# A four-layer diffusion step on one core: three more weight units outside the ring, half an adaLN third in layer 1, the first combine between gate and up, attention's second halves as Q, Q, K, K

## The chip, the core and the metric

The kernel runs on one core of a Trainium2 chip. TensorE (PE in the profile) does the matmuls and transposes, VectorE (DVE) and ScalarE (ACT) the elementwise work, GpSimd (POOL) and SyncE (SP) issue transfers. The metric is device time in microseconds of one execution.

## The reference, cut to what matters

Two sequences of 128 tokens with 1024 channels (context and latent) pass through four layers. Layer i has one token mixer (0 and 3: pooling, 1: attention with 16 heads, 2: Fourier mixing) and then a mixture of 16 experts, of which each token uses two of one group of four. Both are pre-normed and modulated by six rows of 1024 that a product of SiLU(cond) with `ada_w[i]` gives (adaLN).

```python
mod = (cond_act @ ada_w[i] + ada_b[i])[:, None, :]
sh1, sc1, g1, sh2, sc2, g2 = [mod[..., n * D:(n + 1) * D] for n in range(6)]
h = rms_norm(x, norm1_g[i]) * (1 + sc1) + sh1
m = pool_mix(...) or na_context/na_latent(...) or fourier_mix(...)
x = x + g1 * m
h = rms_norm(x, norm2_g[i]) * (1 + sc2) + sh2
x = x + g2 * moe(h, router_w, router_b, moe_w_gate[i], moe_w_up[i], moe_w_down[i])
```

All weights are float32: 24 MB of adaLN a layer, 16 MB for attention in all, and 96 MB of experts a layer. Every weight is read once.

## The kernel before

**Units and the ring.** Weights come in units of 128 partitions x 2048 floats (1024 KB). SyncE issues them in one order that is written out by hand, into a ring of 12 slots; a slot is loaded again when TensorE has counted its former unit as used (`s_used`). `BEFORE_EXPERTS[l]` lists the units ahead of a layer's experts: a third of an adaLN matrix is 8 units (`ada_units(t)`, thirds 3l, 3l+1 and 3l+2 belong to layer l), a block of 512 columns of a 1024-row matrix is 2. Then come four groups of four experts, 24 units each (`GROUP_UNITS`: gate and up in two halves each, down in two). In the first group of a layer three units go to buffers outside the ring: index 0 to `spare`, 7 to `xh` ("rows") and 9 to `hT` ("channels"); SyncE issues the last two behind the first twelve ring units, when the router has read those buffers.

**adaLN.** `ada(t, a, b)` (L1396) multiplies units a to b of third t into bank `B_ADA`; `ada_rows` (L978) adds the bias into `rows`, `ada_turn` (L1413) transposes it, and `ada_mods` (L993, L1001) writes `mods` and `amul` and signals `s_mod`, for which the scaling behind the norm waits (`modulated`: L677 on ScalarE, L969 on VectorE). `FILLS` says which units are computed at a layer's start: some ahead of the last combine of the layer before, some behind it, some behind the transposes. Third 3 (layer 1's first) is computed whole in layer 0's router, L1396 at 95.6 and 102.2 us.

**A layer's start.** The last `combine` (L1927) adds the last expert's output in PSUM; ScalarE and VectorE take the sums of squares, `norm_chain` makes the scale (L935 to L941), the rows are scaled into `xh` (L652, L950), TensorE transposes them in four quarters (`normed`, L1427) and they are modulated into `hT`. Between combine and transposes TensorE runs fill units and 14 transposes that nobody reads (`keep_busy`, L1408). The fourth quarter goes to bank 0, which the first quarter used, and waits until ScalarE has read that.

**Attention (layer 1).** Projections by `by_channel` (L1535: Q0, K0, Q1A, Q1B, K1A, K1B) and `by_token` (L1544: V0, V1A, V1B) alternate with the steps of eight pairs of heads: `scores` (L1562), `bias_max` (L1053 to L1056) and `exps` (L733), `normalise` (L1061, L1064), `turn` (L1571), `copy_turned` (L742), `attend` (L1581), `copy_output` (L1069). adaLN units fill the gaps. A projection's bank is copied out by `empty`, on ScalarE (L722) or VectorE (L1043), as `JOBS` says.

**Experts.** In a group (`group`) the tokens are gathered (L1855), then for each expert gate and up (L1869, L1871) go to one bank in two halves, ScalarE copies the bank to `gu` (L841), TensorE transposes it (`turn`, L1898), SiLU and product follow, then `down` (L1915), the scaling (L1319), a split into high and low parts (L854, L1328) and the `combine` (L1927). The order around the change is

```python
gate_up(2, 0)
turn(1)
combine(0, it8)
gate_up(2, 1)
gate_up(3, 0)   # waits until ScalarE has copied expert 2's bank
```

**GpSimd's queue** loads biases and constants; some wait for the norms' counts (`s_ms`) or the router's (`s_pos`), because their buffers lie over attention's.

Of the kernel before, what the change touches and what calls it, by code (L numbers as in the profile page):

```python
# [7 lines left out]
F32 = mybir.dt.float32  # L8
F32R = mybir.dt.float32r
I32 = mybir.dt.int32  # L10
ALU = mybir.AluOpType
# [42 lines left out]
def matrix_units(name, c):  # L54
# [14 lines left out]
FILLS = {1: (4, [0, 1, 3, 4]), 2: (9, [0, 1, 3, 3]), 3: (11, [0, 1, 3, 4])}  # L69
# [11 lines left out]
SIDES = {0: "spare", 7: "rows", 9: "channels"}  # L81
SIDE_UNITS = {GROUP_UNITS[i]: side for i, side in SIDES.items()}
RING_UNITS = [i for i in range(NU) if i not in SIDES]

# [12 lines left out]
def place(u, l):  # L97

    v = u - EXPERTS_AT[l]
    return u - len(SIDES) * l - sum(1 for i in SIDES if i < v)  # L100


def place_later(u, l):

    return u - len(SIDES) * (l + 1)


USE_OF = {}
for _l in range(DEPTH):
    for _u in range(FIRST_OF_LAYER[_l], EXPERTS_AT[_l] + NU):  # L110
        if _u - EXPERTS_AT[_l] not in SIDES:
            USE_OF[place(_u, _l)] = _u
# [15 lines left out]
HT_BANKS = [[0, 1, 2, 0], [B_ACC, B_ACC + 1, B_ACC + 2, B_ACC + 3]]  # L128
# [84 lines left out]
def build(nc, x_prompt, x_sample, cache_k, cache_v, c, c_ctx, ada_w, ada_b, norm1_g, norm2_g, pool_w,  # L213
# [4 lines left out]
    with ctx:  # L218
# [114 lines left out]
        sides = {"spare": spare[:, :], "rows": xh[:, :, :].rearrange("p s d -> p (s d)"),  # L333
                 "channels": hT[:, :, :].rearrange("p b t -> p (b t)")}
        with ExitStack() as fr:
# [8 lines left out]
            psr_last = sb("psr_last", [P, 512], F32, fr)  # L344

        psr = {0: psr_first, DEPTH - 1: psr_last}
# [16 lines left out]
        s_used = sem("s_used")  # L363
        s_issue = sem("s_issue")
        s_adab = [sem(f"s_adab{k}") for k in range(2)]
        s_psr = sem("s_psr")
        s_rows = sem("s_rows")
        s_adat = sem("s_adat")
# [85 lines left out]
        Q0, K0, FLIPS, CK_TURNS, K_TURN0, V0, Q1A, K1A, Q1B, K1B, V1A, K_TURN1, V1B = 0, 2, 4, 8, 10, 11, 13, 14, 15, 16, 17, 18, 19  # L454
# [9 lines left out]
        SUM_BANKS = [0, 1, 2, 0]  # L464
# [10 lines left out]
        def _(sp):  # L475
# [29 lines left out]
            def load_side(i, l):  # L505
                kind, e, h = GROUP_UNITS[i]
                side = SIDES[i]
# [46 lines left out]
        def _(pool):  # L554
# [56 lines left out]
            pool.wait_ge(s_ms, 4)  # L611
            pool.dma_start(kfour[:, :], k_four).then_inc(s_kc, 16)
            nc.gpsimd.memset(psr[DEPTH - 1][:, :], 0.0).then_inc(s_zero, 1)
            pool.wait_ge(s_zero, 5)
# [10 lines left out]
        def _(ac):  # L625
# [90 lines left out]
            def attention(l, base):  # L716
# [44 lines left out]
                exps(3)  # L761

                copy_turned(3)
# [1237 lines left out]
```

## Time and profile before

| | us |
|---|---|
| median of 3 runs (lowest, highest) | 1355.74 (1353.94, 1356.75) |
| the profiled execution | 1354.35 |
| its span, from first to last instruction | 1352.5 |
| TensorE busy in it | 1267.3 |
| VectorE, ScalarE, GpSimd busy | 391.5, 328.6, 39.3 |
| moved by transfers | 535.21 MB, mean 396 GB/s |

Read the share of an engine only together with what its waits were for, and read the transfers by stretch: a slice of the page is 33.8 us long. In the chain of work that ended last, TensorE has 84% of the span and transfers 9%.

### The profile page before, as it was taken

The page shows a single profiled execution, that of the slowest core. Times are in us where ns is not written, and L with a number is a line of the kernel's source. Part 1 is how long each engine was busy: PE and PEld are TensorE (multiplying, and loading weights), DVE is VectorE, ACT ScalarE, POOL GpSimd, SP SyncE. Part 2 cuts the span into 40 slices and gives each one's busy share as a digit, 9 for nine tenths or more (in the row PEclk, how much of TensorE's full clock was granted, in tenths as well). Part 3 has the DMA queues.
Part 4 walks back from the last instruction along what each step waited for, and adds up shares of the span by engine and source line. Part 5 has one row for each costly group of instructions (what it writes and reads, how often), then busy time and mean ns, then how long its engine had stood idle before and what let it go on. Part 6 is the DMA issues. An engine that isn't in the chain of part 4 may idle for free.

```text
span 1352.5 us, 18262 instructions
## 1 busy us (share of the span) xinstructions
PE 1267.3 (94%) x6665; PEld 576.3 (43%) x6665; DVE 391.5 (29%) x873; ACT 328.6 (24%) x692; POOL 39.3 (3%) x77
## 2 busy tenths in 40 slices
PE   3877999999999998999999999999999999999996
PEld 0433344343657544443433464443434354434342
DVE  1241222132233314222231413321322443213224
ACT  1231122121322223221221323221212452212122
POOL 3010000000000001000000000000000000000000
PEclk9878999999999999999999999999999999999999
DMA  9999999999997899899999998899999999999995
GB/s 374 419 418 421 420 422 421 423 421 421 343 381 310 324 413 402 340 412 420 421 422 422 418 377 326 339 398 420 422 422 422 415 421 363 405 422 421 421 422 227
DMA packets 87260, 535.21 MB, mean 396 GB/s; under 512 B 11192, under 2 KB 13336, under 8 KB 25760
## 3 DMA queue, kind: packets, MB, share of 16 engines
q1 hardware_dynamic: 82336, 527.47, 95.6%
q0 software_dynamic: 3120, 5.23, 1.2%
q10 hardware_dynamic: 1744, 1.73, 0.4%
q8 instruction: 36, 0.59, 0.2%
q14 instruction: 24, 0.20, 0.0%
HBM read 532.26 MB, written 2.12 MB: 395 GB/s over the span
## 4 chain that ended last, share of the span: by engine, by line
PE 84%; DMA 9%; DVE 4%; ACT 2%; issue 1%; SPq 0%; DVEq 0%; ACTq 0%
PE ps L1869 32%; PE ps L1915 15%; DMA ring<-in_ada_w_dram 5%; PE ps L1855 5%; PE ps L1927 5%; PE ps L1535 4%; PE ps L1499 4%; PE ps L1396 4%; PE ps L1898 3%; PE ps L1544 2%; DMA xh<-in_moe_w_up_dram 2%; DMA ring<-in_attn_wqkv_dram 2%; PE ps L1471 1%; PE ps L1886 1%; PE ps L1705 1%
## 5 line engine op out<-in xcount | busy, mean ns | idle before, releaser
L1869 PE MATMUL ps<-ring,xg 128*64 128x512 f32 x992 | 454.2, 601 | 19.6 <-ACT gu L841 12.3
L1871 PE MATMUL ps<-ring,xg 128*64 128x512 f32 x992 | 451.4, 598 | 0.0
L1869 PEld LDWEIGHTS ps<-ring,xg 128*64 128x64 f32 x992 | 127.6, 137 | 275.2 <-issue 248.2
L1915 PE MATMUL ps<-ring,gb 128*64 128x512 f32 x992 | 225.4, 595 | 0.0
L1319 DVE SCALAR_TENSOR_TENSOR gb<-ps,gslot,g2x 128x512 f32<-128x512 f32 x128 | 90.2, 746 | 257.1 <-PE ps L1915 257.1
L1871 PEld LDWEIGHTS ps<-ring,xg 128*64 128x64 f32 x992 | 126.9, 136 | 0.0
L1915 PEld LDWEIGHTS ps<-ring,gb 128*64 128x64 f32 x992 | 68.4, 137 | 132.2 <-issue 124.6
L854 ACT ACTIVATE y_hi<-gb 128x512 fp32r<-128x512 f32 x128 | 77.1, 626 | 168.3 <-PE ps L1927 108.4
L1396 PE MATMUL ps<-ring,cact 128*32 128x512 f32 x768 | 92.9, 617 | 10.3 <-ACT cact L638 5.3
L841 ACT ACTIVATE gu<-ps 128x512 f32<-128x512 f32 x64 | 38.3, 598 | 231.8 <-PE ps L1871 231.8
L1328 DVE TENSOR_TENSOR y_lo<-gb,y_hi 128x512 fp32r<-128x512 f32 x128 | 83.5, 688 | 12.5 <-ACT y_hi L854 11.9
L1310 DVE TENSOR_TENSOR gb<-sg,ps 128x256 f32<-128x256 f32 x64 | 26.8, 418 | 202.8 <-ACT sg L846 202.8
L846 ACT ACTIVATE sg<-ps 128x256 f32<-128x256 f32 x64 | 24.5, 383 | 209.6 <-PE ps L1898 209.6
L837 ACT ACTIVATE xg<-ps 128x512 f32<-128x512 f32 x64 | 38.2, 597 | 117.8 <-PE ps L1855 117.7
L1927 PE MATMUL ps<-y_hi,onehotT 64*128 64x512 f32 x256 | 57.6, 447 | 3.1 <-DVE y_lo L1328 3.1
L1336 DVE TENSOR_TENSOR gpair<-onehotT 128x8 f32<-128x8 f32 x16 | 2.7, 167 | 191.1 <-ACT onehotT L860 191.1
L1535 PE MATMUL ps<-hT,ring 128*128 128x256 f32 x256 | 56.6, 381 | 1.1 <-DMA ring<-in_attn_wqkv_dram 1.1
L1855 PE MATMUL ps<-onehot,h_hi 128*128 128x256 f32 x256 | 54.9, 296 | 0.5 <-DVE amul L1001 0.5
L1535 PEld LDWEIGHTS ps<-hT,ring 128*128 128x128 f32 x256 | 48.2, 190 | 9.0 <-issue 2.6
L1855 PE MATMUL ps<-onehot,h_lo 128*128 128x256 f32 x256 | 51.3, 282 | 0.0
L1396 PEld LDWEIGHTS ps<-ring,cact 128*32 128x32 f32 x768 | 21.9, 112 | 67.9 <-issue 51.5
L1927 PE MATMUL ps<-y_lo,onehotT 64*128 64x512 f32 x256 | 50.3, 390 | 0.0
(211 smaller groups left out, 1092.8 us busy)
## 6 DMA issues: line engine op xcount, KB each, us to landing
ring<-in_moe_w_up_dram SPq DMA_DIRECT2D x124, 1024.0 KB, 14.8
ring<-in_moe_w_gate_dram SPq DMA_DIRECT2D x124, 1024.0 KB, 13.6
ring<-in_moe_w_down_dram SPq DMA_DIRECT2D x124, 1024.0 KB, 15.4
ring<-in_ada_w_dram SPq DMA_DIRECT2D x96, 1024.0 KB, 17.8
ring<-in_attn_wqkv_dram SPq DMA_DIRECT2D x12, 1024.0 KB, 19.9
spare<-in_moe_w_gate_dram SPq DMA_DIRECT2D x4, 1024.0 KB, 18.8
xh<-in_moe_w_up_dram SPq DMA_DIRECT2D x4, 1024.0 KB, 12.5
hT<-in_moe_w_down_dram SPq DMA_DIRECT2D x4, 1024.0 KB, 13.8
```

The source lines that it names most:

```text
L854: nc.scalar.activation(y_hi[:, s, :], y[:, s, :], ACT.Copy).then_inc(s_yh, 1)
L1319: v.scalar_tensor_tensor(y[:, s, :], ps[:, DOWN_BANKS[e % 2], :], gslot[:, e:e + 1], g2x[:, s, :], ALU.mult, ALU.mult).then_inc(s_yf, 1)
L1328: v.tensor_tensor(y_lo[:, s, :], y[:, s, :], y_hi[:, s, :].bitcast(F32), ALU.subtract).then_inc(s_y, 1)
L1396: mm = pe.matmul(ps[32 * j:32 * (j + 1), B_ADA, :], cact[:, i, :], w[:, j * 512:(j + 1) * 512], start=(i == 0), stop=(i == ADA_UNITS - 1))
L1499: mm = pe.matmul(ps[:, banks[2 * cc + s], :], src[4 * h + b][:, s * SEQ:(s + 1) * SEQ], w[:, b * 512:(b + 1) * 512], start=(h == 0 and b = ...
L1535: mm = pe.matmul(ps[:, JOB_BANK[i], d * T:(d + 1) * T], w[b // 4][:, at:at + P], hT[:, b, :], start=(b == 0), stop=(b == DB - 1))
L1855: mm = pe.matmul(ps[:, (B_G, B_T)[j % 2], d * 256:(d + 1) * 256], h[:, s, b * P:(b + 1) * P], onehot[:, s, :, 0:SLOTS], start=(n2 == 0), s ...
L1869: mg = pe.matmul(ps[0:SLOTS, B_GU, :], xg[:, b, e, :], wg[:, i * F:(i + 1) * F], start=(b == 0), stop=(b == DB - 1))
L1871: mu = pe.matmul(ps[SLOTS:P, B_GU, :], xg[:, b, e, :], wu[:, i * F:(i + 1) * F], start=(b == 0), stop=(b == DB - 1))
L1898: mm = pe.transpose(ps[:, B_T, j * P:(j + 1) * P], gu[:, j, :], ident)
L1915: mm = pe.matmul(ps[r * SLOTS:(r + 1) * SLOTS, DOWN_BANKS[e % 2], :], acts[:, e % ACTS, j, :], w[:, i * D + r * HALF:i * D + (r + 1) * HAL ...
L1927: mm = pe.matmul(ps[:, B_ACC + 2 * s + r, :], onehotT[part, NSEQ * e + s, 0:SEQ], of[part, s, :], start=False, stop=False, skip_group_chec ...
```

## The change

- Layer 0 computes only units 0 to 3 of adaLN third 3 in its router; VectorE adds their sum to the bias row (`ada_begun`), and TensorE waits for that before the gather, because the bank is used again. Units 4 to 7 are layer 1's first fill (one ahead of the last combine, three behind it). There the row, turn and `mods` of third 3 come between the norm and the scaling; the turn stands ahead of the last quarter of the transposes. Layer 1's former four fill units (third 4) move into attention. Layer 2's fill has five units ahead of the Fourier sums in place of three.
- `keep_busy(14)` stays only ahead of layer 3.
- The last quarter of the transposes (and of the Fourier sums) goes to another bank and waits for VectorE's copy out of it in place of ScalarE's read of the first.
- In layers 1 to 3 the first group's units 1, 2 and 3 go outside the ring too: to `gb`, to a buffer over `onehotT`, `gu` and `sg`, and to one over the constants. SyncE issues them behind eight ring units, after waiting for the last residual addition and for the cache's writes. Constants that share the third buffer are loaded when it has been used (`s_behind`); pooling scales of layer 3 are loaded into `grow`.
- Attention's second halves run Q1A, Q1B, K1A, K1B with other steps between them, and adaLN units are placed anew: two that stood behind V1B stand later.
- `combine(0)` stands between `gate_up(2, 1)` and `gate_up(3, 0)`.

```diff
-    ada_units(0) + [("pool", 0, 0)] + ada_units(1) + ada_units(2) + ada_units(3),
-    ada_units(4)[:4] + matrix_units("qkv", 0) + matrix_units("qkv", 2) + ada_units(4)[4:]
-    + matrix_units("qkv", 4) + ada_units(5) + matrix_units("qkv", 1) + matrix_units("qkv", 3) + ada_units(6)
+    ada_units(0) + [("pool", 0, 0)] + ada_units(1) + ada_units(2) + ada_units(3)[:4],
+    ada_units(3)[4:] + matrix_units("qkv", 0) + matrix_units("qkv", 2) + ada_units(4)
+    + matrix_units("qkv", 4) + ada_units(5) + matrix_units("qkv", 1) + ada_units(6)[:4] + matrix_units("qkv", 3) + ada_units(6)[4:]
...
-FILLS = {1: (4, [0, 1, 3, 4]), 2: (9, [0, 1, 3, 3]), 3: (11, [0, 1, 3, 4])}
+FILLS = {1: (3, [4, 5, 8, 8]), 2: (9, [0, 1, 5, 5]), 3: (11, [0, 1, 3, 4])}
...
-SIDES = {0: "spare", 7: "rows", 9: "channels"}
+SIDES = [{0: "spare", 7: "rows", 9: "channels"}] + [
+    {0: "spare", 1: "gates", 2: "turned", 3: "behind", 7: "rows", 9: "channels"}] * (DEPTH - 1)
+AHEAD_OF_SIDES = 8
...
-HT_BANKS = [[0, 1, 2, 0], [B_ACC, B_ACC + 1, B_ACC + 2, B_ACC + 3]]
+HT_BANKS = [[0, 1, 2, B_ACC + 2], [B_ACC, B_ACC + 1, B_ACC + 2, B_ACC + 3]]
...
             def first_group(l, base):
                 load_side(0, l)
-                for n, i in enumerate(RING_UNITS):
+                for n, i in enumerate(RING_UNITS[l]):
+                    if n == AHEAD_OF_SIDES and l > 0:
+
+                        sp.wait_ge(s_xr, 4 * (l + 1))
+                        sp.wait_ge(s_kv, 32)
+                        load_side(1, l)
+                        load_side(2, l)
+                        load_side(3, l)
...
-            pool.wait_ge(s_ms, 4)
+            pool.wait_ge(s_behind, 1)
             pool.dma_start(kfour[:, :], k_four).then_inc(s_kc, 16)
...
-            pool.wait_ge(s_ms, 6)
+            pool.wait_ge(s_behind, 2)
...
-            pool.wait_ge(s_pos, DEPTH)
+            pool.wait_ge(s_behind, DEPTH - 1)
...
+            def ada_begun(t, l, base):
+
+                v.wait_ge(s_used, used(UNIT_AT[("ada", t, 3)], l, base))
+                v.wait_ge(s_adab[t % 2], 64 * (t // 2 + 1))
+                v.tensor_tensor(adabr[:, t % 2, :], ps[:, B_ADA, :], adabr[:, t % 2, :], ALU.add).then_inc(s_begun, 1)
+                v.wait_ge(s_begun, 1)
...
                     norm_chain(2 * l)
                     normed_rows()
+                    if l == 1:
+                        ada_rows(3, l, base)
+                        ada_mods(3)
...
                 if l == 0:
-                    ada_rows(3, 0, 0)
-                    ada_mods(3)
+                    ada_begun(3, 0, 0)
...
-                    if n % 2 == 0 and j == 3:
-                        pe.wait_ge(s_ha, 2 * TURNED_BEFORE[n] + 1)
+                    if j == 3:
+                        if between is not None:
+                            between()
+                        if n % 2 == 0 and n > 0:
+                            pe.wait_ge(s_xd, n)
...
-                ada(4, 4, ADA_UNITS, l, base)
+                ada(4, 0, ADA_UNITS, l, base)
...
-                w, wk = weights(1), weights(3)
+                w = weights(1)
                 by_channel(Q1A, w, 0)
 
                 ada_turn(5)
                 turn(2)
                 scores(3)
                 attend(1)
-                by_channel(K1A, wk, 0)
-
+                by_channel(Q1B, w, 1)
+
+                ada(6, 0, 4, l, base)
                 turn(3)
-                emptied(Q1A)
+                attend(2)
+                w = weights(3)
+                by_channel(K1A, w, 0)
+
+                attend(3)
+                emptied(Q1B)
                 emptied(K1A)
                 scores(4)
-                attend(2)
-                by_channel(Q1B, w, 1)
+                by_channel(K1B, w, 1)
...
                 turned(K_TURN1, [kT[:, 4 + i, 0:SEQ] for i in range(4)])
-
-                scores(7)
                 ada_turn(6)
                 by_token(V1B, w, 1)
-                ada(7, 0, 2, l, base)
+
                 emptied(V1A)
                 emptied(V1B)
                 attend(4)
                 turn(6)
+                scores(7)
                 attend(5)
-                ada(7, 2, 4, l, base)
+                ada(7, 0, 6, l, base)
                 turn(7)
...
                 begin(2)
                 if l == 0:
-                    ada(3, 4, ADA_UNITS, l, base)
-                    ada_turn(3)
-                    pe.wait_ge(s_mod, 4)
+                    pe.wait_ge(s_begun, 1)
...
                     turn(1)
+                    gate_up(2, 1)
                     combine(0, it8)
-                    gate_up(2, 1)
                     gate_up(3, 0)
...
                     fill(l + 1, 1, base)
-                    keep_busy(14)
+                    if l == 2:
+                        keep_busy(14)
```

## Rows read from the trace of the kernel before

**Rows 1.** The profile page, parts 1, 2 and 6.

```profile
PE 1267.3 (94%) x6665; PEld 576.3 (43%) x6665; DVE 391.5 (29%) x873; ACT 328.6 (24%) x692; POOL 39.3 (3%) x77
...
GB/s 374 419 418 421 420 422 421 423 421 421 343 381 310 324 413 402 340 412 420 421 422 422 418 377 326 339 398 420 422 422 422 415 421 363 405 422 421 421 422 227
...
xh<-in_moe_w_up_dram SPq DMA_DIRECT2D x4, 1024.0 KB, 12.5
```

**Rows 2.** The chain that ended last, whole span: start us, us, what.

```profile
106.27 25.43 DMA xh<-in_moe_w_up_dram
...
593.93 1.13 PE ps L1927 x8
...
649.37 1.13 PE ps L1927 x8
...
751.41 26.01 DMA ring<-in_ada_w_dram
...
1053.02 21.98 DMA ring<-in_ada_w_dram
```

**Rows 3.** Windows of attention, of layer 1's first experts, of the end.

```profile
431.00:442.00 11.00, 10.82 (x80) 9.16 (x80) 3.65 (x9) 3.93 (x11) 0.00 (x0) 1.00 0.10 16
...
452.00:520.00 68.00, 68.00 (x348) 29.18 (x341) 14.27 (x31) 13.72 (x34) 5.21 (x10) 1.00 1.02 411
...
545.00:555.00 10.00, 10.00 (x58) 5.02 (x56) 1.03 (x4) 2.88 (x6) 0.00 (x0) 1.00 0.62 203
...
565.00:580.00 15.00, 14.28 (x72) 5.13 (x70) 3.09 (x6) 2.62 (x5) 0.00 (x0) 1.00 0.97 370
...
1332.00:1337.00 5.00, 5.00 (x29) 1.74 (x26) 3.40 (x7) 1.76 (x4) 0.00 (x0) 1.00 0.49 203
```

**Rows 4.** Waits of TensorE, whole span: us in total, times, longest.

```profile
PE ps L1869 <- ACT gu L841: 12.3, 16, 0.9
...
PE ps L1869 <- DMA xh<-in_moe_w_up_dram: 7.3, 1, 7.3
...
PE ps L1396 <- DMA ring<-in_ada_w_dram: 3.5, 4, 1.6
```

**Rows 5.** Timeline, 102 to 108 us, layer 0: start us, us, instruction.

```profile
102.19 3.64 PE L1396 MATMUL ps<-ring,cact 128*32 128x512 f32 x32
...
105.96 0.69 DVE L978 TENSOR_TENSOR rows<-ps,adabr 128x512 f32<-128x512 f32 x1 [1.35 <-PE ps L1396]
...
107.85 0.39 PE L1855 MATMUL ps<-onehot,h_hi 128*128 128x256 f32 x1 [0.49 <-DVE amul L1001]
```

**Rows 6.** Windows: busy us of PE, PEld, DVE, ACT, POOL, clock, DMA, GB/s.

```profile
132.00:140.00 8.00, 8.00 (x26) 2.62 (x27) 0.00 (x0) 0.60 (x1) 0.00 (x0) 0.64 1.02 423
...
1107.00:1111.00 4.00, 1.98 (x24) 1.23 (x23) 2.73 (x9) 3.98 (x10) 0.00 (x0) 0.94 1.00 418
...
1111.00:1115.00 4.00, 4.00 (x21) 3.71 (x21) 2.17 (x10) 2.63 (x6) 0.00 (x0) 0.64 1.02 424
```

**Rows 7.** Timeline, 342 to 380 us, layer 1's start.

```profile
343.03 1.06 PE L1396 MATMUL ps<-ring,cact 128*32 128x512 f32 x8 [0.32 <-DMA ring<-in_ada_w_dram]
...
346.74 2.90 ACT L677 ACTIVATE hT<-ps,mods,amul 128x128 f32<-128x128 f32 x8 [0.23 <-PE ps L1427]
...
351.03 27.86 PE L1535 MATMUL ps<-hT,ring 128*128 128x256 f32 x128 [1.08 <-DMA ring<-in_attn_wqkv_dram]
```

**Rows 8.** Timeline, 441 to 492 us, attention, VectorE.

```profile
467.11 0.42 DVE L1053 TENSOR_REDUCE r_ge<-ps 128x2 f32<-128x256 f32 x1 [6.51 <-PE ps L1562]
...
470.80 1.03 DVE L1064 TENSOR_TENSOR soft<-soft,r_ge 128x256 f32<-128x256 f32 x2
...
474.56 0.69 DVE L1043 COPY vtok<-ps 128x512 f32<-128x512 f32 x1 [2.73 <-PE ps L1544]
```

**Rows 9.** Timeline, 530 to 565 us: the unit in xh.

```profile
534.19 0.33 SPq L508 DMA_DIRECT2D xh<-in_moe_w_up_dram  x1
...
557.26 0.64 PE L1871 MATMUL ps<-xh,xg 128*64 128x512 f32 x1
```

More of the change, by code:

```diff
@@ L78, with side_landed @@
 LAYER_UNITS = NG * NU
-SIDES = {0: "spare", 7: "rows", 9: "channels"}
-SIDE_UNITS = {GROUP_UNITS[i]: side for i, side in SIDES.items()}
-RING_UNITS = [i for i in range(NU) if i not in SIDES]
+SIDES = [{0: "spare", 7: "rows", 9: "channels"}] + [
+    {0: "spare", 1: "gates", 2: "turned", 3: "behind", 7: "rows", 9: "channels"}] * (DEPTH - 1)
+SIDE_UNITS = [{GROUP_UNITS[i]: side for i, side in of.items()} for of in SIDES]
+RING_UNITS = [[i for i in range(NU) if i not in of] for of in SIDES]
+SIDES_BEFORE = [sum(len(of) for of in SIDES[:l]) for l in range(DEPTH + 1)]
+AHEAD_OF_SIDES = 8
+def side_landed(side, l):
+    return 16 * sum(1 for of in SIDES[:l + 1] if side in of.values())
 UNIT_AT, EXPERTS_AT, FIRST_OF_LAYER = {}, [], []
@@ L99, in place @@
     v = u - EXPERTS_AT[l]
-    return u - len(SIDES) * l - sum(1 for i in SIDES if i < v)
+    return u - SIDES_BEFORE[l] - sum(1 for i in SIDES[l] if i < v)
 def place_later(u, l):
-    return u - len(SIDES) * (l + 1)
+    return u - SIDES_BEFORE[l + 1]
 USE_OF = {}
@@ L332, in build @@
             gain = sb("gain", [P, D], F32, last)
-        sides = {"spare": spare[:, :], "rows": xh[:, :, :].rearrange("p s d -> p (s d)"),
+        with ExitStack() as sd:
+            sb("sd_before", [P, 11 * D], F32, sd)
+            turned_side = sb("turned_side", [P, UNIT], F32, sd)
+        with ExitStack() as bh:
+            sb("bh_experts", [P, 13 * D + 64], F32, bh)
+            behind = sb("behind", [P, UNIT], F32, bh)
+        sides = {"gates": gb[:, :, :].rearrange("p s d -> p (s d)"), "turned": turned_side[:, :], "behind": behind[:, :],
+                 "spare": spare[:, :], "rows": xh[:, :, :].rearrange("p s d -> p (s d)"),
                  "channels": hT[:, :, :].rearrange("p b t -> p (b t)")}
@@ L1097, in attention @@
                 normalise(3)
[L1098 removed]
+                empty(Q1B, blocks(qT, 6, 2))
+                copy_output(2)
+                copy_output(3)
                 bias_max(4)
[L1101 removed]
                 normalise(4)
+                empty(K1B, blocks(kT, 6, 2))
                 bias_max(5)
[L1105 removed]
                 normalise(5)
[L1107 removed]
+                ada_rows(6, l, base)
                 bias_max(6)
[L1110 removed]
                 normalise(6)
+                ada_mods(6)
+                empty(V1B, vtok[:, 1, 512:1024])
+                copy_output(4)
                 bias_max(7)
[L1114 removed]
+                copy_output(5)
                 normalise(7)
[L1116 to L1118 removed]
+                copy_output(6)
+                copy_output(7)
                 ada_rows(7, l, base)
@@ L1414, in ada_turn, with normed @@
                 mm.then_inc(s_adat, 1)
-            def normed(n):
+            def normed(n, between=None):
                 for j in range(4):
@@ L1887, in turn_onehots @@
                                            start=True, stop=True)
+                            if i == 0 and first and l > 0:
+                                mm.then_inc(s_behind, 1)
                             if i % 3 == 2 or i == GROUP * NSEQ - 1:
```

60 lines of the change are left out of this document (24 added, 36 removed).

## The prediction, on record before the result

> **What bounds the kernel now.** I read the page first [rows 1]: TensorE is busy 1267.3 of 1352.5 us, and transfers run at about 420 GB/s in most slices. Both are nearly full, so of every edit the question is which of the two ends last where the edit sits. A weight unit is 1024 KB; at 422 GB/s it takes 1,048,576 / 422,000 = 2.485 us. A group of four experts takes 24 units, 59.6 us of transfers; TensorE passes through one in 649.37 - 593.93 = 55.44 us [rows 2]. So in an expert stage TensorE gains 4.2 us a group on the stream, and in the mixers, where it works long on few units, the stream catches up until the ring is full. Then it starves: 16 GB/s in 431 to 442 us [rows 3].
>
> The list of waits [rows 4] shows what that leaves. TensorE waits once 7.3 us for the unit in `xh`, 3.5 us in four pieces for adaLN units, and 12.3 us in 16 pieces (0.77 each, one a group) for ScalarE's copy of `gu`. The chain [rows 2] passes through a DMA at 106.27 (that unit, layer 0), at 751.41 and at 1053.02 (adaLN units behind the experts of layers 1 and 2). So layer 0 is bound by transfers, and the later layers by TensorE, with the stream just in time at the end of each. What only quickens TensorE among the experts is therefore paid in part.
>
> **Layer 0: four units fewer.** Half of adaLN third 3 leaves the stream ahead of the experts: 4 x 2.485 = 9.9 us. TensorE must be there in time. It loses the adaLN work (3.64 us at 102.19) and the turn, but still waits for VectorE, which is free at 105.96 - 1.35 = 104.61, adds the partial row in 0.69 and signals: the gather starts near 105.4, not at 107.85 [rows 5]. TensorE wanted the `xh` unit at 131.7 - 7.3 = 124.4 [rows 2, 4]; now it wants it at 122.0, and that lands at 131.7 - 9.9 = 121.8. Its new idle 3.2 us (102.2 to 105.4) may halve the clock for a while; that is covered, because the 7.3 us wait goes and with it the slow stretch behind it (0.64 over 8 us, 8 x 0.36 = 2.9 us lost [rows 6]). At the layer's end the stream decides: **-9.9**.
>
> **Start of layer 1.** The four units are now its first. One is computed ahead of the last combine, three behind it, and they arrive 2.485 us apart while each takes 1.06 [rows 7]. Before, the third adaLN unit there was begun when it landed, at 343.03; the fourth lands 2.5 later, 9.9 earlier by the shift: 335.6, and is done at 336.6. Then follow the addition, the turn and two VectorE operations, 107.85 - 105.96 = 1.9 us in layer 0 [rows 5], up to 0.9 more because the turn stands behind twelve transposes, the eight scalings of 2.90 us, and 0.3 for semaphores: 342.6 for the first QKV matmul, against 351.03 [rows 7]. That is -8.4, so **+1.5** is lost. The last quarter of the transposes goes to another bank and waits no more; ScalarE's chain hides it: 0.
>
> The busy transposes are gone here, and TensorE has 1 us of work in 2.5 for three units, then 3 us of none. With 1.98 us of work in the 4 us from 1107 the granted clock was 0.64 in the next 4 [rows 6], that is, part of it at 1.2 GHz: 4 x 0.36 = 1.4 us lost. Here it is from 0 (the drop missed) to 2.9 + 1.4 = 4.3; I take **+2.5**, since the gap is longer than that at 1107 and the work behind it dense. The Trainium skill (TensorE: Matmul & The Clock Gate, What's actually happening) says that the half rate is the default and activity releases it; by it I should count near the upper end, +4. The rows agree that the clock falls and leave the length open.
>
> **Attention.** Hardly anything in it waits (68.00 of 68 us busy [rows 3]), so the order Q, Q, K, K can't make TensorE faster; it frees slots earlier where the stream starves. It must only add no waits. From a score to its normalised rows VectorE and ScalarE take 470.80 + 1.03 - 467.11 = 4.7 us [rows 8]; between each score and its turn stands a projection (27.86 / 4 = 7.0 us [rows 7]) or six adaLN units (6 x 0.9) and an attend. K1A's copy hides under attend 3. One wait is bare: behind the second half of V, adaLN work hid VectorE's copy (0.69 [rows 8]); now the attend follows at once: +0.9 with semaphores. And the four moved units cost here what they take, 4 x 0.9 = 3.6. Together **+4.5**. The weights arrive in time: the stream is 1.5 us further ahead of TensorE than before.
>
> **Three more units outside the ring.** They let the stream run on at the end of the mixer. It moves 203 GB/s in 545 to 555 us and 370 in 565 to 580 [rows 3], starving for slots. Yet the units behind the first eighteen need the same ring slots, which the same matmuls free; with or without the sides the stream is full there and restarts on the same releases, a little smoother: 15 x 50 / 420 = 1.8 us less lost at most, and 0.5 as the first combine releases two slots earlier. From 0.3 to 2.3 a layer; I take 1.3.
>
> **First combine behind the up half.** The combine's 1.13 us [rows 2] covers the 0.77, so TensorE gains 3.1 us a layer. In layer 0 the stream takes it all. In layers 1 and 2 the stream is just in time and allows what it gained itself: **-1.3** each. In layer 3 no weights follow; the stream ends near 1332 + 5 x 203 / 422 = 1334.4 [rows 3], some 1.8 us ahead of need: -1.3 - 1.8 = **-3.1**, at best 4 x 0.9 = 3.6.
>
> **Start of layer 2.** Four adaLN units come at the stream's pace ahead of the Fourier sums, without busy transposes; the last unit (751.41 + 26.01 [rows 2]) still decides when the spectra start. One stretch at half clock would cost 1.4: **+0.5**, from 0 to 1.4.
>
> Constants on POOL's queue wait for the third side unit and fall where the stream starves; they are needed a layer later: 0. SP's wait for the last residual addition stands where the next slots aren't free either: 0.
>
> **Sum** against the profiled execution: -9.9 + 1.5 + 2.5 + 4.5 - 1.3 + 0.5 - 1.3 - 3.1 = -6.6. Its span of 1352.5 becomes 1345.9 and its time of 1354.35 becomes 1347.8. The runs' median is 1.4 above that execution: 1355.74 - 6.6 = 1349.1, rounded **1349**.
>
> The Trainium skill (DMA: Bandwidth & Descriptors, Specifications) puts HBM's limit for one core near 358 GB/s, by which four units would be 11.7 us and the time 1347; the trace shows 420 [rows 1], and the measurement decides.
>
> **The rivals.**
> *The clock stays up and the stream uses its sides well.* No half clock (-3.0 against the sum), 2.3 in place of 1.3 in layers 1 and 2, 3.6 in layer 3: -12.1 in all, 1343.6. For it: all stretches of [rows 3] hold 1.00. Against it: [rows 6].
> *Eaten up.* Half clock for 4.3 us in layer 1 and 1.4 in layer 2, and 0.3 from the stream in each layer (2.1 in the last): -9.9 + 1.5 + 4.3 + 4.5 - 0.3 + 1.4 - 0.3 - 2.1 = -0.9, 1354.8. For it: the waits that vanish are TensorE's, and the stream bounds three of four layer ends [rows 2].
> *Slower: the unit in `xh` comes late in layers 1 to 3.* The three sides stand ahead of it. In layer 1 it is issued at 534.19, lands 12.5 later and is used at 557.26 [rows 1, 9]: 10.6 us of slack, of which three units take 7.5. If the stream is more than 3.1 us behind my count TensorE stalls, and as in layer 0 the clock falls behind the stall. With 2.0 of stall and 1.4 of clock in three layers that is +10.2, so +3.6: 1359.3. It makes the kernel slower from 1.7 us of stall a layer. Against it: in 545 to 555 us the stream has run dry [rows 3], some 7 us before that unit is used.
> *The combine covers nothing*, because the wait moves to another engine: then mainly layer 3 loses, 1.8: 1351, inside the forecast's range.
>
> **How the numbers follow.** The forecast has 0.54 (its own range 1345 to 1352.5, from the clock's and the stream's bounds), the good rival 0.24, eaten up 0.13, slower 0.09. Less than 0.2% (2.7 us) can hardly be told from no change with this kernel, so faster means under 1353.0: faster 0.78, same 0.13, slower 0.09. The range reaches into the good rival and to the third: 1341.5 to 1355.5.
>
> **What would show it.** Right: the wait for `xh` in layer 0 under 1 us; the 16 waits for `gu` gone; the first QKV matmul 6 to 9 us earlier, with a slow clock before or behind it; layer 1's first gather 1 to 4 us earlier; new short waits for DMA at the ends of layers 0 to 2; 0.9 us ahead of one attend. Wrong: layer 0 ending less than 9 us earlier (then TensorE bounded it); waits for `xh` in layers 1 to 3; groups 3 us a layer shorter with no wait for DMA at the ends of layers 1 and 2 (then the sides give the lead that I deny them).

## The result, and the profile after

The changed kernel takes 1349.17 us (median of 6 executions, 1343.44 to 1352.03) against 1356.68 for the kernel before (6 executions, 1353.94 to 1358.48): 7.5 us or 0.6% less, ratio 0.994 with a 95% interval of 0.9921 to 0.9958. Forecast were 1349.0 and 6.6 us less. One execution of the kernel before (5961.67 us) and one of a variant (2621.9 us) were in a slow state, and no range or interval below has them.

The profiled execution of the changed kernel is the quickest of the six: 1343.44 us, its span 1341.6, 10.9 less than the span of before. The median stands 5.7 us above it. So one part of what follows asks what the change gave, another why its executions differ.

The page after, parts 1 and 2, in the form of [rows 1]:

```profile
span 1341.6 us, 18222 instructions
...
PE 1260.9 (94%) x6637; PEld 570.9 (43%) x6637; DVE 391.5 (29%) x874; ACT 328.2 (24%) x692; POOL 38.8 (3%) x76
...
GB/s 372 420 418 421 421 421 422 422 422 418 338 410 408 334 354 391 340 421 421 422 422 421 418 385 317 345 404 421 422 422 421 415 420 387 407 421 422 422 422 250
```

TensorE's busy time is 6.4 us shorter (28 unread transposes less, and less of it at half clock) and its waits 4.5 us. The transfers run at the same 420 GB/s. What changed is which waits are left. TensorE's waits after, in the form of [rows 4]:

```profile
PE ps L1432 <- DMA ring<-in_ada_w_dram: 8.1, 8, 1.6
...
PE ps L1908 <- DMA ring<-in_moe_w_up_dram: 4.3, 7, 1.3
...
PE ps L1908 <- DMA xh<-in_moe_w_up_dram: 3.2, 1, 3.2
PE ps L1969 <- DVE y_lo L1365: 3.1, 4, 1.5
PE ps L1894 <- DVE adabr L1018: 3.1, 1, 3.1
PE ps L1574 <- ACT hT L702: 3.0, 1, 3.0
...
PE ps L1957 <- DMA ring<-in_moe_w_down_dram: 1.3, 4, 0.3
```

The 12.3 us for ScalarE's copy of `gu` are gone. In their place stand waits for weights among the experts (4.3 and 1.3 us, where before there were none but that for `xh`, which has shrunk from 7.3 to 3.2) and 4.6 us more for adaLN units. The chain that ended last, in the form of [rows 2], shows where:

```profile
96.00 26.08 DMA xh<-in_moe_w_up_dram
...
283.36 22.49 DMA ring<-in_moe_w_up_dram
310.07 25.62 DMA ring<-in_ada_w_dram
...
716.14 20.02 DMA ring<-in_moe_w_up_dram
739.95 23.59 DMA ring<-in_ada_w_dram
...
1044.08 23.55 DMA ring<-in_ada_w_dram
...
1299.10 22.81 DMA ring<-in_moe_w_down_dram
```

Now every layer ends with a transfer, layer 3 too: the chain goes through a down unit that lands at 1299.10 + 22.81 = 1321.91, 20 us ahead of the end. Before, it went through none in layer 3.

The start of layer 1 and the one bare wait of attention, in the timeline, as in [rows 7, 8]:

```profile
333.23 1.07 PE L1432 MATMUL ps<-ring,cact 128*32 128x512 f32 x8 [0.53 <-DMA ring<-in_ada_w_dram]
335.74 1.07 PE L1432 MATMUL ps<-ring,cact 128*32 128x512 f32 x8 [1.44 <-DMA ring<-in_ada_w_dram]
...
342.13 8.04 PE L1574 MATMUL ps<-hT,ring 128*128 128x256 f32 x36 [2.99 <-ACT hT L702]
...
468.79 0.66 PE L1620 MATMUL ps<-pT,vtok 128*64 128x128 f32 x8 [0.83 <-issue]
```

The last adaLN unit is begun when it has landed, at 335.74 (335.6 in the working), and the first projection starts at 342.13 (342.6). And the projections start at full clock here: 1.00 from 340 to 348, where I had counted 2.5 us for half a clock.

### The profile page after: what moved, and what is told of

It reads as the page before. It is cut to its first block, busy times and chain, and to the rows that moved or that the text cites. A ratio compares the mean times of both kernels' runs of the same rounds, so it can differ in the third digit from the quotient of the medians.

```text
span 1341.6 us, 18222 instructions
## 1 busy us (share of the span) xinstructions
PE 1260.9 (94%) x6637; PEld 570.9 (43%) x6637; DVE 391.5 (29%) x874; ACT 328.2 (24%) x692; POOL 38.8 (3%) x76
## 3 DMA queue, kind: packets, MB, share of 16 engines
q10 hardware_dynamic: 1744, 1.73, 0.4%
## 4 chain that ended last, share of the span: by engine, by line
PE 79%; DMA 14%; DVE 4%; ACT 2%; issue 1%; SPq 0%; DVEq 0%; ACTq 0%
PE ps L1908 29%; PE ps L1957 13%; DMA ring<-in_ada_w_dram 7%; PE ps L1894 5%; PE ps L1969 4%; PE ps L1432 4%; PE ps L1574 4%; PE ps L1538 4%; DMA ring<-in_moe_w_up_dram 3%; PE ps L1940 2%; PE ps L1583 2%; DMA xh<-in_moe_w_up_dram 2%; DMA ring<-in_moe_w_down_dram 2%; PE ps L1510 1%; PE ps L1925 1%; PE ps L1746 1%
## 5 line engine op out<-in xcount | busy, mean ns | idle before, releaser
L1908 PE MATMUL ps<-ring,xg 128*64 128x512 f32 x968 | 441.9, 599 | 7.5 <-DMA ring<-in_moe_w_up_dram 4.3
L1910 PE MATMUL ps<-ring,xg 128*64 128x512 f32 x944 | 429.9, 598 | 0.0
L1908 PEld LDWEIGHTS ps<-ring,xg 128*64 128x64 f32 x968 | 124.2, 137 | 245.5 <-issue 233.6
L1910 PEld LDWEIGHTS ps<-ring,xg 128*64 128x64 f32 x944 | 120.9, 137 | 0.0
L871 ACT ACTIVATE sg<-ps 128x256 f32<-128x256 f32 x64 | 24.5, 383 | 216.1 <-PE ps L1940 216.1
```

What stands on the lines that cost most here:

```text
L1908: mg = pe.matmul(ps[0:SLOTS, B_GU, :], xg[:, b, e, :], wg[:, i * F:(i + 1) * F], start=(b == 0), stop=(b == DB - 1))
L1910: mu = pe.matmul(ps[SLOTS:P, B_GU, :], xg[:, b, e, :], wu[:, i * F:(i + 1) * F], start=(b == 0), stop=(b == DB - 1))
```

## The experiments

Each was timed against the kernel before in the same rounds on one chip, whose medians there were 1357.4, 1357.0, 1356.6 and 1356.5 us in four sets. The changed kernel itself ran in the first and the last of these sets alone; where a run of another set is held against it, the two come from different sets. "First gather" is the first matmul of a layer's gather; it marks the end of its mixer and router.

**The same kernel again, twice.** No edit.

> The changed kernel once more, unchanged. Its six times lie between 1343.44 and 1352.03 us, and the profiled one is the lowest of them, with a mean granted clock of 0.987; the others had 0.980 to 0.986. Theory (clock): what differs between its executions is stretches of TensorE at the lower of its two clock levels; the start of layer 1 (333 to 352 us), which stayed at 1.00 in the profiled execution, is one of them in others. Then the median of the new times is 1349 (1347 to 1351), and times and mean clocks go together, some 1 us for each 0.001. Rival (transfers): the spread comes from the stream, then the clock of the times is the same for slow and quick ones.

> The changed kernel once more, on the same chip and in the same rounds as the run below, so that the two can be compared directly. Theory (the clock falls in some executions behind the waits that the change opened): a median of 1349 (1347.5 to 1350.5), a spread of 5 us or more, and a fall of the granted clock at one or more of 340 to 348, 764 to 772, 844 to 852 and 1104 to 1116 us. Rival (it was the chips of the earlier runs): within 1 us of the run below.

Measured: 1349.43 us (1346.39 to 1353.32, ratio 0.995, interval 0.9931 to 0.9968) and 1347.94 (1345.03 to 1351.95, ratio 0.9936, interval 0.9918 to 0.9954). The profiled executions took 1348.30 and 1349.78 us. Windows of the profile of the first result, of the first repeat and of the second (columns as in [rows 6]; the granted clock is the third from the right):

```profile
344.00:348.00 4.00, 4.00 (x20) 3.54 (x19) 0.00 (x0) 0.00 (x0) 0.00 (x0) 1.00 1.08 253
764.00:768.00 4.00, 4.00 (x24) 2.55 (x17) 0.00 (x0) 0.55 (x3) 0.00 (x0) 0.62 1.01 420
848.00:852.00 4.00, 4.00 (x28) 2.48 (x26) 0.00 (x0) 0.60 (x2) 0.00 (x0) 1.00 1.01 418
```

```profile
344.00:348.00 4.00, 4.00 (x20) 3.54 (x19) 0.00 (x0) 0.00 (x0) 0.00 (x0) 1.00 1.06 244
764.00:768.00 4.00, 3.56 (x16) 1.90 (x17) 0.00 (x0) 0.00 (x0) 0.00 (x0) 0.50 1.02 424
768.00:772.00 4.00, 4.00 (x26) 4.00 (x25) 1.30 (x5) 1.74 (x7) 0.00 (x0) 0.65 0.99 386
844.00:848.00 4.00, 3.96 (x15) 2.43 (x15) 3.76 (x12) 0.00 (x0) 0.00 (x0) 0.73 1.02 426
```

```profile
344.00:348.00 4.00, 4.00 (x16) 3.38 (x15) 0.00 (x0) 0.00 (x0) 0.00 (x0) 0.77 1.08 275
768.00:772.00 4.00, 4.00 (x22) 3.95 (x19) 0.05 (x1) 1.14 (x4) 0.00 (x0) 0.50 1.02 415
848.00:852.00 4.00, 4.00 (x20) 3.35 (x20) 2.67 (x15) 0.71 (x2) 0.00 (x0) 0.62 1.01 424
```

Both expectations hold for the median. Over the 18 executions of the changed kernel the time goes with the mean granted clock: the seven at 0.981 or less took 1349.64 to 1353.32 us, the eleven at 0.983 or more 1343.44 to 1349.20. That is some 0.6 us for each 0.001, where I had 1, and the rival of equal clocks is out.

One program, one order of instructions, and the clock does not fall at the same places each time: at 764 us in all three, but for longer in the repeats; at 844 to 852 us in the repeats alone; at 340 to 348 us in the second repeat alone. Stage by stage, in us against the profile of before (from the starts of the first projection and of the first gathers, 351.03, 540.6, 849.8, 1119.3, and the span):

| stage | forecast | result's profile | repeat 1 | repeat 2 |
|---|---|---|---|---|
| start to first projection | -8.4 | -8.9 | -8.9 | -8.6 |
| to layer 1's first gather | +7.0 | +3.5 | +3.6 | +5.2 |
| to layer 2's | -0.8 | -0.4 | +1.8 | +1.6 |
| to layer 3's | -1.3 | -2.3 | -0.1 | -0.3 |
| to the end | -3.1 | -2.8 | -2.4 | -2.4 |
| sum | -6.6 | -10.9 | -6.0 | -4.5 |

The first stage and the last agree in all three within 0.4 us. The three between differ where the clock does. In attention the clock of the second repeat held back 4 x (0.19 + 0.23) = 1.7 us at 340 to 348, and it is 1.6 us longer. From layer 1's last weight unit to layer 2's first gather, where the clock falls at 764, it takes 92.9, 94.3 and 94.3 us, against 92.3 before and in the filled kernels below whose clock stays up. From layer 2's first gather to its last unit it takes 216.1, 218.3 and 218.1 us; only in the repeats does the clock fall there. The kernel before has a fall of its own in its profile, at 1108 to 1116 us ([rows 6] show it); from layer 2's last unit to layer 3's first gather it takes 51.8 us, and the changed kernel, without a fall there, 51.1 in all three.

**The first combine alone, and all but it.**

```diff
-                    combine(0, it8)
                     gate_up(2, 1)
+                    combine(0, it8)
                     gate_up(3, 0)
```

made in the kernel before:

> The kernel before with nothing changed but the place of the first combine. Theory (the stream ends the layers): TensorE gains 3.1 us a layer, the stream gives none of it in layer 0, up to 0.9 in layer 1, 0.1 in layer 2, and 1.8 to 3.1 in layer 3; the time falls by 1.8 to 4.1 us, likeliest 2.9, and waits for weights of 2 to 3 us appear ahead of the ends of layers 1 and 2. Rival 1 (TensorE ends the layers): it falls by 12.3 us. Rival 2 (the wait only moves to another place): 0, and the waits of TensorE for the copy or another engine stay at some 12 us.

and undone in the changed kernel:

> The changed kernel with the first combine ahead of the second gate_up of expert 2 again. TensorE waits 16 times 0.77 us for ScalarE's copy. Theory (the stream ends the layers): layer 0 has 6.4 us of waits for weights to take up its 3.1, layer 1 some 4, layer 2 1.6, layer 3 0.6; so the median rises by 0 + 0 + 1.5 + 2.5 = 4.0 us (2.5 to 5.5). Rival (TensorE ends the layers): by 12.3 us.

Measured: alone 1354.11 us (1351.36 to 1356.25, ratio 0.9978, interval 0.9969 to 0.9988), 3.3 less. Undone 1353.39 (1351.21 to 1355.17), 4.0 more than the changed kernel in the same rounds (1349.43). Both are in the stream theory's range, and 12.3 it is not. Where TensorE's gain went is one view, its waits with the combine alone:

```profile
PE ps L1869 <- DMA xh<-in_moe_w_up_dram: 11.8, 1, 11.8
PE ps L1869 <- DMA ring<-in_moe_w_up_dram: 7.4, 13, 1.0
...
PE ps L1915 <- DMA ring<-in_moe_w_down_dram: 1.2, 4, 0.3
```

There is no row for `gu` any more, so the wait did not move to another engine. The 12.3 us of waits for ScalarE left, and 7.4 + 1.2 us of waits for the experts' units came, and 0.9 for adaLN units (4.4 against 3.5). (The wait for `xh` stands ahead of the first moved combine; it is longer because layer 0's first gather came at 104.0 us in this execution, not at 107.9.) The last unit of layers 0 to 3 lands at 335.97, 757.61, 1067.98 and 1336.03 us, against 335.52, 757.47, 1067.53 and 1336.04 before: not one layer's stream moved. The span is 1.7 us shorter, all of it behind that last landing. The 3.3 of the medians are more than the 1.7 of the profiles; before's profiled execution is 2 to 3 us under its medians.

**The half third alone**, in the kernel before (order of attention, combine, sides and banks as before):

```diff
-    ada_units(0) + [("pool", 0, 0)] + ada_units(1) + ada_units(2) + ada_units(3),
-    ada_units(4)[:4] + matrix_units("qkv", 0) + matrix_units("qkv", 2) + ada_units(4)[4:]
+    ada_units(0) + [("pool", 0, 0)] + ada_units(1) + ada_units(2) + ada_units(3)[:4],
+    ada_units(3)[4:] + matrix_units("qkv", 0) + matrix_units("qkv", 2) + ada_units(4)
...
-FILLS = {1: (4, [0, 1, 3, 4]), ...
+FILLS = {1: (3, [4, 5, 8, 8]), ...
...
-                    keep_busy(14)
+                    if l > 0:
+                        keep_busy(14)
```

> The kernel before with the half third alone: units 4 to 7 of adaLN third 3 computed at the start of layer 1, its former fill units in attention, no transposes ahead of layer 1; the attention's old order, the first combine in its old place, no more sides. By the terms of the prediction: -9.9 + 1.5 + 3.6 = -4.8, and up to 2.5 less with a half clock at layer 1's start: 1352.5 to 1355.0 against 1357.3. Rival (attention's new order is what pays for the units there): layer 1's stretch from the first QKV matmul to the gather, 189.6 us in the kernel before, becomes over 194 us, against 193.1 in the changed kernel, and the time falls by less than 3 us.

Measured: 1352.88 us (1352.37 to 1355.11, ratio 0.9974, interval 0.9964 to 0.9984), 4.1 less than 1357.0, as forecast. From the first projection (343.31) to the gather (538.9) are 195.6 us, more than the rival's 194, but with the clock at 0.50 from 344 to 348 us and at 0.91 from 348 to 352, both filled by TensorE:

```profile
340.00:344.00 4.00, 1.34 (x6) 1.04 (x7) 2.33 (x8) 3.47 (x10) 2.22 (x4) 0.74 1.06 387
344.00:348.00 4.00, 4.00 (x11) 3.19 (x10) 0.00 (x0) 0.00 (x0) 1.41 (x2) 0.50 1.09 373
348.00:352.00 4.00, 4.00 (x18) 3.43 (x18) 0.00 (x0) 0.00 (x0) 0.00 (x0) 0.91 0.99 251
```

That held back 4 x (0.50 + 0.09) = 2.4 us, and up to 0.3 more ahead of 344. At full clock it would be, by this estimate, 192.9 to 193.2, and the changed kernel has 193.1. The new order of attention gains nothing that shows; no run undid it by itself. The old bank shows in this run: 2.03 us ahead of the last quarter and 1.51 ahead of the projection, 3.5 together where the changed kernel waits 2.99.

```profile
341.15 0.66 PE L1439 MATMUL ps<-const,xh 128*128 128x128 f32 x4 [2.03 <-ACT hT L678]
343.31 7.00 PE L1547 MATMUL ps<-hT,ring 128*128 128x256 f32 x19 [1.51 <-DVE hT L970]
```

**Without the sides.**

```diff
-SIDES = [{0: "spare", 7: "rows", 9: "channels"}] + [
-    {0: "spare", 1: "gates", 2: "turned", 3: "behind", 7: "rows", 9: "channels"}] * (DEPTH - 1)
+SIDES = [{0: "spare", 7: "rows", 9: "channels"}] * DEPTH
```

> The changed kernel with units 1, 2 and 3 of each first group in the ring again, in layers 1 to 3. My theory (the ring's slots are freed by the same matmuls either way; the sides only smooth the restart): the median rises by 0.9 to 6.9 us, likeliest 3.9, that is 1.3 a layer. Rival 1 (the sides give three units of lead, 7.5 us of transfers a layer, and so carry the whole combine gain of 3.1 us a layer): it rises by 7 to 12 us, with long waits for weights at the ends of layers 1 to 3. Rival 2 (they do nothing): 0 to 0.9.

(Their `load_side` calls go too; SyncE's two waits ahead of them and the constants' later loads stay.) Measured: 1347.95 us (1345.36 to 1351.46, ratio 0.9935, interval 0.9919 to 0.9951), 1.5 less than the changed kernel in the same rounds. My 3.9 us for the sides was wrong; they give nothing that the times can show, which is nearest to rival 2. The profile of the first result says why. In layer 2 SyncE issues the sides at 828 to 829 us. From 786 to 809 the full ring had held it, and from 802 to 810 the stream moved only 41 GB/s:

```profile
785.46 0.57 SPq L528 DMA_DIRECT2D spare<-in_moe_w_gate_dram  x1
809.14 0.33 SPq L497 DMA_DIRECT2D ring<-in_moe_w_gate_dram  x1
...
828.09 0.33 SPq L528 DMA_DIRECT2D gb<-in_moe_w_up_dram  x1
828.77 0.33 SPq L528 DMA_DIRECT2D turned_side<-in_moe_w_gate_dram  x1
```

```profile
802.00:810.00 8.00, 8.00 (x29) 3.29 (x32) 0.82 (x2) 1.28 (x4) 0.00 (x0) 1.00 0.10 41
```

So I tried one of them earlier.

**One side ahead of the full ring.**

```diff
                 load_side(0, l)
+                if l > 1:
+                    sp.wait_ge(s_xd, 2 * l)
+                    load_side(2, l)
...
-                        load_side(2, l)
+                        if l == 1:
+                            load_side(2, l)
```

> The changed kernel with one of the three new sides (unit 2, over onehotT, gu and sg) issued in layers 2 and 3 right behind side 0 in place of behind eight ring units. Theory (a side is worth something only if it is issued before the ring is full): the stream's idle time of 7.3 us at 802 to 810 us shrinks by 2.5; layer 2 ends 1.6 us earlier, by the waits for weights that it has at its end, and layer 3 up to 0.6: median 1347 to 1348 (from 1349.3). Rival 1 (the same slots are freed by the same matmuls and the lead is lost by the end of the first group): 1349.3 within 1 us and the same waits for weights at the end of layer 2. Rival 2 (the unit takes transfers from the ring's units, adaLN's last ones above all): layer 2's first gather, 844.0 us, comes later.

Measured: 1351.81 us (1346.87 to 1352.39, ratio 0.9957, interval 0.9943 to 0.9971), no gain. It is even 2.5 us above the changed kernel's median of another set, which none of the three theories has; the mean granted clocks of its six executions, 0.978 to 0.983, are low, but why is not shown. The side goes out at 788.23 and fills part of the hole. The first repeat of the changed kernel is the one to compare with, because layer 2's first gather comes at the same time there (846.27 us, here 846.25): from 798 to 816 us the stream moves 282 GB/s where it moved 183, but from 852 to 864 it moves 154 where it moved 230. First this run, then the repeat:

```profile
798.00:816.00 18.00, 18.00 (x67) 6.68 (x66) 2.77 (x4) 2.99 (x7) 0.00 (x0) 1.00 0.71 282
852.00:864.00 12.00, 12.00 (x68) 5.95 (x68) 2.29 (x7) 3.27 (x7) 0.57 (x1) 1.00 0.44 154
```

```profile
798.00:816.00 18.00, 18.00 (x67) 6.68 (x66) 2.77 (x4) 2.99 (x7) 0.00 (x0) 1.00 0.48 183
852.00:864.00 12.00, 12.00 (x65) 5.42 (x62) 1.87 (x6) 2.89 (x6) 0.57 (x1) 1.00 0.56 230
```

The lead is given back as soon as the ring is full again, in the first group. Rival 2 is out: from layer 1's last unit to layer 2's first gather it takes 92.7 us, no more than the 92.9 to 94.3 of the changed kernel. From layer 2's first gather to the landing of its last unit are 216.5 us, 216.1 in the result's profile. That distance hardly varies: over the profiles of the changed kernel and the variants that keep its combine and sides, where the clock did not fall at the first gather, it is 215.6 to 217.2 us in layers 1 to 3, and 216.0 to 217.4 without the sides. So a layer's end follows from when its experts begin.

**The waits filled.** Transposes that nobody reads, in the waits that the change opened. First try:

```diff
-                ada(t, ends[part], ends[part + 1], l, base)
+                for i in range(ends[part], ends[part + 1]):
+                    if part == 1 and l < 3 and i > ends[part]:
+                        keep_busy(3 if i == ends[part] + 1 else 10)
+                    ada(t, i, i + 1, l, base)
...
+                if l in (1, 3):
+                    sums_out(l)
+                    keep_busy(22 if l == 1 else 13, B_ACC + 1)
...
+                if l > 0:
+                    pe.wait_ge(s_g2x, 2 * l + 2)
+                    keep_busy(12)
```

and in the same way 6 ahead of the second norms' transposes in layers 1 and 2 and 5 ahead of the ranks.

> The changed kernel with transposes that nobody reads in the waits of TensorE at the starts of layers 1 to 3 and in their routers: 3 and 10 between the adaLN units that it waits for, 22 ahead of layer 1's first projection, 6, 12 and 5 in the later waits, each shorter than the wait that it fills. Theory (the clock): short work between waits lets the granted clock fall in some executions; in three profiles it fell to 0.50 to 0.84 at 340 to 348, 764 to 772, 844 to 852 or 1104 to 1116 us, in each at other ones of these. Then the profile shows 1.00 at all four, and the median falls from 1349.3 to 1344 to 1346.5 with a spread under 6 us (8.6 before). Rival 1 (the fall comes whatever TensorE does there): the same 1349.3 within 1 us, with falls left. Rival 2 (the transposes delay what stands behind them): 1350 to 1353, with a clock of 1.00.

Measured: 1354.62 us (1351.88 to 1356.48, ratio 0.9982, interval 0.9973 to 0.9991), some 5 more than the changed kernel and nearest to rival 2. The transposes ahead of the projection use a bank of the accumulators, and had to wait until ScalarE had copied it:

```profile
342.72 3.73 PE L1447 MATMUL ps<-const 128*128 128x128 f32 x22 [3.97 <-ACT x L692]
346.25 4.01 PE L1577 MATMUL ps<-hT,ring 128*128 128x256 f32 x15
...
1110.31 1.53 PE L1447 MATMUL ps<-const 128*128 128x128 f32 x12 [2.72 <-ACT g2x L715]
```

The projection comes 4.1 us later, and in layer 3 the transposes wait 2.72 and 1.73 us. But the clock is at 1.00 at 764, 844 and 1108 us; it falls once behind the experts of layer 0, to 0.57 at 344, behind the longest of the new waits. So the second try takes a bank that needs no wait (`B_ACC + 3`) for layer 1, and leaves layer 3's two places out:

```diff
-                if l in (1, 3):
-                    sums_out(l)
-                    keep_busy(22 if l == 1 else 13, B_ACC + 1)
+                if l == 1:
+                    keep_busy(22, B_ACC + 3)
...
-                if l > 0:
-                    pe.wait_ge(s_g2x, 2 * l + 2)
+                if l in (1, 2):
                     keep_busy(12)
```

> The changed kernel with transposes that nobody reads in its waits, this time without any wait of their own: 3 and 10 between the adaLN units at the starts of layers 1 and 2, 22 (2.8 us) ahead of layer 1's first projection in a bank that needs no copy of ScalarE's, 6 ahead of the second norms' transposes and 12 ahead of the router in layers 1 and 2, 5 ahead of the ranks in layers 1 to 3. Theory (in the run before, the waits for ScalarE cost 4.1 us at layer 1's start and some 4 in layer 3, and hid what the clock gave): first projection at 342 us again, granted clock 1.00 in all stretches from 333 to 1100 us, median 1344 to 1347 against 1349.3. Rival 1 (what the clock gives back, the transposes take from the work behind them): 1348 to 1351 with the clock at 1.00. Rival 2 (the clock falls in spite of them): falls as before, 1349.3 or more.

then with `ada(7, 0, 2)` back behind `by_token(V1B)`:

> The run above with two adaLN units back behind the second half of V, as cover for VectorE's copy. In the changed kernel TensorE stands there 0.83 us (at 468.0). Theory (TensorE sets the attention's length): that wait goes, layer 1's gather comes 0.8 us earlier and with it the end: 0.8 us under the run above. Rival (the ring is full less long and the stream gives the gain back at the layer's end): gather 0.8 earlier, last unit of layer 1 at the same time, 0 to 0.3 us.

then that without the sides:

> The run above with units 1, 2 and 3 of each first group in the ring again. Theory (the sides are worth 0 to 0.4 us a layer, as the distance from a layer's first gather to the landing of its last unit says: 216.1 us on the mean with them, 216.6 without): 0 to 1.5 us over the run above. Rival (three units of lead): 3 us or more over it.

and the last once more, beside the second repeat of the changed kernel:

> The changed kernel with transposes in its waits, two adaLN units as cover behind the second half of V, and no new sides, once more. Theory (the clock): 1344 to 1346, a spread of 3 us, no fall of the granted clock between 333 and 1100 us; 4 to 5 us under the run above. Rival (chance of the earlier runs): within 1 us of it.

| kernel | us, median (range) | ratio to before, 95% |
|---|---|---|
| filled | 1345.90 (1344.64 to 1349.24) | 0.9924 (0.9911 to 0.9937) |
| and V1B covered | 1345.64 (1344.87 to 1348.81) | 0.9922 (0.9909 to 0.9935) |
| and no sides | 1344.54 (1344.19 to 1346.60) | 0.9914 (0.9901 to 0.9927) |
| the same again | 1345.09 (1343.56 to 1348.20) | 0.9916 (0.9901 to 0.9932) |

The last row against 1347.94 in the same rounds is 2.9 us, less than the 4 to 5 that I expected, and its spread is 4.6 us, not 3. This comparison changes the sides as well as the fill. With the sides as they are on both, the fill is worth 1345.8 (10 executions) against 1348.8 (18), 3.0 us; without sides on both 1344.8 (11) against 1347.95 (6), 3.2 us. Some 3 us is what the fill gives; by the ratios to before, which compare within a set, it is 2.6 to 2.7. Taking the sides out gave 1.1 us here (third row against second), where I expected it to cost 0 to 1.5, and 1.5 in the run without the sides: they don't help, and whether they cost something lies within the spread. All four medians are below those of the kernel before and of the changed one. The profiles of all but the second show the clock at 1.00 from 333 us to the end of the last group, and of the 21 executions none has a mean granted clock under 0.984, where the changed kernel goes down to 0.977. In the windows where the repeats fell, the last of the four:

```profile
344.00:348.00 4.00, 4.00 (x20) 3.51 (x20) 0.00 (x0) 0.00 (x0) 0.00 (x0) 1.00 1.05 287
764.00:768.00 4.00, 4.00 (x37) 3.29 (x30) 1.12 (x4) 1.45 (x6) 0.00 (x0) 1.00 1.01 420
848.00:852.00 4.00, 4.00 (x28) 2.48 (x26) 0.00 (x0) 1.02 (x2) 0.00 (x0) 1.00 0.43 107
```

The second fell at 1100 to 1108 us, in layer 3's router, whose longest wait is not filled. So rival 1 is out: the fill costs less than the clock gives back, when it waits for nothing itself. The cover behind V1B is a miss for the theory, though. The wait of 0.83 us is gone, and a new one of 0.45 stands nine microseconds later, for VectorE's normalised rows, which now have four adaLN units ahead of them in place of six:

```profile
477.09 0.87 PE L1613 MATMUL ps<-const,soft 128*128 128x128 f32 x6 [0.45 <-DVE soft L1096]
```

From first projection to gather it is 192.9 us in place of 193.1, and the time is 0.3 us less than in the row above, where the theory had 0.8.

## Why the prediction was right, and where only its sum was

**Layer 0, -9.9: right.** Its last unit lands at 325.74 us in place of 335.52, 9.8 earlier, 9.8 and 9.4 in the repeats. TensorE's own times there were off, and with them one of my signs: the wait for `xh` was to be under 1 us. The first gather is at 100.9 where I had 105.4, because VectorE was free at 100.2; in the second repeat, with a slower clock in the router, it is at 105.4. The unit in `xh` was waited for 3.2, 2.9 and 0 us, and the layer ended within 0.4 us of the same time, although the mean granted clock up to 330 us was 0.96, 0.97 and 0.95, 3 to 7 us of TensorE's time apart. That is what bound by transfers means: a slow clock costs nothing there.

**Start of layer 1, +1.5: right** (+1.0 by -8.9 against -9.9). The bank that I counted as nothing gives half a microsecond, by the half third alone (3.5 against 2.99).

**Attention, +4.5: found 3.5.** Four units at 0.9 are the whole of it. The bare wait of 0.83 is where I put it, but the stretch isn't longer for it; covering it only uncovered another. The order of the halves is worth 0, as forecast, as far as the half third alone shows. Because the half clock did not come there (2.5), the stretch was 1 us shorter than forecast and started 0.5 earlier, layer 1's first gather came 5.3, 5.3 and 3.4 us earlier; my sign of 1 to 4 held only with the slow clock of the second repeat.

**Half clock, +2.5 in layer 1 and +0.5 in layer 2: the mechanism right, place and size not.** At layer 1's start the three profiles give 0, 0 and some 1.6 us (the 5.2 against 3.6 and 3.5 of the table); other variants with the same start fell as well (0.50 at 344 with the combine undone). At layer 2's start the falls cost 0.6, 2.0 and 2.0 us (92.9, 94.3 and 94.3 against 92.3), where I had 0.5; at its first gather they cost nothing in the result's profile and some 2 us in the repeats (218.3 and 218.1 against 216.1), where I had nothing. And I counted from a profile that has a fall itself: the one at 1108 to 1116 us, which is in [rows 6], costs the kernel before 0.7 us (51.8 against 51.1), and the three profiles after lack it. For a median execution the filled kernels give some 3 us, and the 3.0 that I had agrees; since the places and the sizes were others, that is in part luck. Nothing in the runs says which of the places falls in an execution, and so the three sums run from -10.9 to -4.5. The Trainium skill (TensorE: Matmul & The Clock Gate, What's actually happening) says that the half rate is the default and activity holds it off; the filled kernels agree, with 1.00 at every place whose wait was filled without a new wait. The same section says that a kernel's first slow stretch varies from run to run; here that holds in the middle of a program too, where a fall comes in one execution and stays out in the next.

**Sides, part of -1.3 a layer: failed.** "They let the stream run on at the end of the mixer" is the step. They don't: they are issued behind the full ring, and a lead gained there is lost in the first group; without them the kernel took 1347.95 us against 1349.43. The sentence in front of my number, that the same matmuls free the same slots, was the whole truth as far as these runs show. With this term at nothing the sum held in part by luck: attention was 1.0 too high the other way.

**Combine, -1.3, -1.3 and -3.1: right in kind.** Layer 3 gives 2.8, 2.4 and 2.4 us. In layers 1 and 2 the gain becomes waits for weights at the end, as forecast. From the first gather to the last unit, layer 1 takes 215.9, 216.7 and 216.5 us against 216.9 before, and layer 2 216.1 in the profile without a fall there, against 217.7: 0.2 to 1.6 us less, where I had 1.3. The combine alone shows 216.6 and 218.1, so which part of the change gives it stays open. Alone, the combine is worth 3.3 us, the half third 4.1: 7.4 together, against 7.5 to 8.5 for the whole change in its three sets.

**Rivals.** "The unit in `xh` comes late" is out: in layer 1 it lands at 546.5 and is used at 551.9, 5.4 us of slack, 5.4 and 1.7 in layers 2 and 3, and no wait. "The clock stays up" is nearly what the quickest execution did, 1343.4 (1343.6 in the working): it has one fall, at 764 us, and its sides gave nothing, so the match of the number is luck. With the waits filled the clock stays up in three profiles of four. "Eaten up", 1354.8, is out: none of the 18 executions took so long. "The combine covers nothing" is out too: the waits that came are for weights, not for another engine.

## What to carry to other kernels

Where two resources are nearly equal, remove a unit from the stage that the stream bounds, and look for the stage whose other engine has room; a gain of the engine that is not last turns into its waits for the other. Buffers that are filled behind a full ring added no lead here, and one filled ahead of it lost its lead in the first group. When an edit opens waits on TensorE, fill them with work that nobody reads and that waits for nothing (some 3 us here; 5 us lost where it waited), and profile several executions before one is called the time.

## What the runs showed of the hardware that was not expected

The granted clock is not a property of the program. Three profiles of one kernel differ by up to 6.4 us in span, and by the granted clock 5.1 us of that is time held back between the first projection and the last group, in stretches at 0.50 to 0.84 behind waits of 0.5 to 3 us: at 764 us in each but for different lengths, at 844 us in two, at 340 us in one. With 3 to 22 transposes in those waits the last profile shows 1.00 from 333 us to the end of the last group. The range over executions is 4.6 us (11, 1343.56 to 1348.20, sides taken out) where the changed kernel's is 9.9 (18, 1343.44 to 1353.32); with the sides in it is 4.6 (10, 1344.64 to 1349.24).
